# A hybrid RWKV-7 / pooling / mixture-of-experts step on one core: the chunk inverses' first level taken by ScalarE instead of VectorE, the key norms taken one number a token, and the state factors as one product a direction

## The reference, cut to what matters

```
kk    = heads(k * k_k);  kk = kk / max(sqrt(sum(kk*kk, -1)), 1e-12)      # key norm, one number a token and head
k_dir = heads(k * (1 + (a - 1) * k_a))
step: sa = s @ kk_t;  s = s * w_t - sa (x) (kk_t * a_t) + v_t (x) k_t;  y = s @ r_t     # per head, both directions
y     = groupnorm(y_f + y_b) * ln_x_w + ln_x_b;  y = (y + bonus) * g
```

## Time and profile before

| | |
|---|---|
| median of 3 runs (lowest to highest) | 3024.35 us (3022.92 to 3027.27) |
| the profiled execution, its span | 3028.03 us, 3026.2 us |
| projection phase, scan phase | 0 to 406 us, 406 to 1167 us |
| output and routing, experts and end | 1167 to 1360 us, 1360 to 3026 us |
| busy over the span: PE, DVE, ACT, POOL | 90%, 40%, 19%, 19% |

### The profile page before, as it was taken

How to read it: one execution, slowest core, us unless ns; L and a number is a source line. 1 busy time by engine, 2 the same in 40 slices (tenths; PEclk the granted TensorE clock), 3 DMA queues, 4 the chain that set the end, 5 groups by cost and what they waited for, 6 DMA issues and landing times. The chain is left out here.

```text
span 3026.2 us, 74869 instructions
## 1 busy us (share of the span) xinstructions
PE 2715.8 (90%) x32716; PEld 2389.9 (79%) x32716; DVE 1214.7 (40%) x3032; ACT 568.8 (19%) x1406; POOL 569.1 (19%) x571
## 2 busy tenths in 40 slices
PE   7999947788878897976999999999999999999991
PEld 2555527777767883446999999999999999999991
DVE  1488565757575453324223321332123222332125
ACT  4010153444342232320000100010000100010002
POOL 0693024534444331000000000000000000000002
PEclk9999979999999998987999999999999999999996
DMA  5522210000001004017687768777787768777753
GB/s 205 165 98 83 84 39 7 3 4 7 4 5 39 5 5 172 28 40 283 259 319 279 266 249 295 265 277 272 253 305 281 272 242 318 271 265 259 279 210 133
DMA packets 235257, 517.92 MB, mean 171 GB/s; under 512 B 9853, under 2 KB 42877, under 8 KB 234938
## 3 DMA queue, kind: packets, MB, share of 16 engines
q1 hardware_dynamic: 224410, 483.14, 43.3%
q0 software_dynamic: 8176, 21.83, 3.0%
q10 hardware_dynamic: 2480, 10.06, 0.8%
HBM read 488.68 MB, written 26.33 MB: 170 GB/s over the span
## 5 line engine op out<-in xcount | busy, mean ns | idle before, releaser
L2275 PE MATMUL ps_h<-xT,w1c 128*128 128x144 f32 x4096 | 547.1, 287 | 1.3 <-ACT xT L2081 1.3
L2275 PE MATMUL ps_h<-xT,w3c 128*128 128x144 f32 x4096 | 544.3, 286 | 0.0
L2275 PEld LDWEIGHTS ps_h<-xT,w1c 128*128 128x128 f32 x4096 | 520.4, 191 | 1.7 <-ACT xT L2081 1.7
L2275 PEld LDWEIGHTS ps_h<-xT,w3c 128*128 128x128 f32 x4096 | 519.9, 190 | 0.0
L2285 PE MATMUL ps_ye<-he,w2c 128*128 128x144 f32 x4096 | 512.3, 286 | 0.0
L2285 PEld LDWEIGHTS ps_ye<-he,w2c 128*128 128x128 f32 x4096 | 505.9, 190 | 0.0
L2230 DVE TENSOR_TENSOR u<-ps_h,sig 128x144 f32<-128x144 f32 x256 | 78.8, 308 | 887.8 <-ACT sig L2112 887.8
L563 PE MATMUL front_bank<-wide,win 128*128 128x384 f32 x912 | 298.9, 490 | 2.0 <-DVE wide L447 2.0
L563 PEld LDWEIGHTS front_bank<-wide,win 128*128 128x128 f32 x912 | 173.8, 191 | 128.2 <-issue 9.9
L2112 ACT ACTIVATE sig<-ps_h 128x144 f32<-128x144 f32 x256 | 74.4, 291 | 1065.8 <-PE ps_h L2275 1065.8
L2143 POOL DMA_INDIRECT acc<-ys,idx_s x16 | 25.8, 1615 | 1002.8 <-ACT ye_p L2101 872.0
(11 more groups left out here) (292 smaller groups left out, 3176.1 us busy)
## 6 DMA issues: line engine op xcount, KB each, us to landing
w1c<-in_w SPq DMA_DIRECT2D x64, 2048.0 KB, 8.1
w3c<-in_w SPq DMA_DIRECT2D x64, 2048.0 KB, 13.0
w2c<-in_w SPq DMA_DIRECT2D x64, 2048.0 KB, 13.4
ada<-in_ada_w SPq DMA_DIRECT2D x24, 1024.0 KB, 6.0
prow<-probsT ACTq DMA_DIRECT2D x17, 576.0 KB, 7.2
...
```

The source lines that it names most:

```text
L2275: ins = eng.matmul(ps_h[g % 2][:, off:off + SLOTS], w[:, b, k, f * P:(f + 1) * P], xT[:, k], start=(k == 0), stop=(k == KT - 1))
```

## The change

Five things, all in the scan phase (the experts' phase only has two counters merged into one).

1. Level 0 of the inverse: GpSimd's `begin_tt` now adds the identity to `lm` in place, one pair ahead, right behind `level(n, 0)`. TensorE's product with the identity then is T whole. ScalarE copies it (`begin_t`) and the transpose (its own `begin_tt`) to `tw`; VectorE's `take_t(n, 0)` is gone.
2. The key norm: a job `ks` a tile multiplies the squares as stationary operand with one column of ones (36 matmuls with one moving column), so that sums stand as 128x9 for each head; two small square roots, then `invert` (floor and reciprocal of 128x18). A job `kb` a piece (12 matmuls of 64x64) spreads the result back over rows and columns, and VectorE's `unit` reads it from PSUM in two products of 128x3x64, and does the product with the rates as before. `unit` runs in the job's spot.
3. `factors` is one product of 128x20 a direction; `rk_b` is gone.
4. The reciprocal of `spread` is three of 128x128.
5. The tables: `ks`, `w`, `a`, `kb` and the norm's jobs at other spots, with a fifth spot (k = 4) at the end of a pair; `exps` and GpSimd's `kr` one place earlier.

```diff
         def jobs(p, k):            # excerpts
-            for lo, name, t in ((0, "w", 0), (3, "a", 0), (6, "kk", 0), (9, "w", 1)):
+            for lo, num, name, t in ((0, 1, "ks", 0), (1, 3, "w", 0), (4, 3, "a", 0), (7, 3, "kb", 0), (10, 3, "w", 1)):
...
-            for name, spots in (("a", ((0, 3), (1, 0), (1, 1))), ("kk", ((1, 2), (1, 3), (2, 0))),
-                                ("bonus", ((3, 1), (3, 2), (3, 3)))):
+            spots = {"ks": ((0, 0),), "w": ((0, 1), (0, 2), (0, 3)) if t > 1 else (), "a": ((1, 0), (1, 1), (1, 2)),
+                     "kb": ((1, 3), (2, 0), (2, 1)), "bonus": ((3, 1), (3, 2), (3, 3))}
...
     @block.gpsimd
         def begin_tt(n):
-            eng.wait_ge(lm_p[n % 2], levels_done(n, 0))
-            if n >= 2:
-                eng.wait_ge(wu_pe, n - 1)
-            eng.tensor_tensor(tw[:, n % 2, :, 1], lm[:, n % 2, 0],
+            eng.wait_ge(lm_p[n % 2], levels_done(n, 0) - 1)
+            eng.tensor_tensor(lm[:, n % 2, 0], lm[:, n % 2, 0],
                               eye.unsqueeze(1).to_broadcast([P, 4, CH]), ALU.add).then_inc(lm_p[n % 2], 1)
...
-                if (r, q) in ((2, 5), (3, 1), (3, 3)):
-                    kr(t, ((2, 5), (3, 1), (3, 3)).index((r, q)))
+                if (r, q) in ((2, 4), (3, 0), (3, 2)):
+                    kr(t, ((2, 4), (3, 0), (3, 2)).index((r, q)))
...
     @block.scalar
+        def begin_t(n):
+            b = n % 2
+            if n >= 2:
+                eng.wait_ge(wu_pe, n - 1)
+            eng.wait_ge(x_pe[b], (n // 2) * LEVELS + 1)
+            eng.activation(tw[:, b, :, 0], INV[b][:, 0:4 * CH].rearrange("p (u c) -> p u c", u=4), ACT.Copy).then_inc(t0_s[b], 1)
+
+        def begin_tt(n):
+            b = n % 2
+            eng.wait_ge(lm_p[b], levels_done(n, 0))
+            eng.activation(tw[:, b, :, 1], lm[:, b, 0], ACT.Copy).then_inc(t0_s[b], 1)
...
-                spots = ((2, 3), (2, 4), (2, 5), (3, 1), (3, 2), (3, 3))
+                spots = ((2, 2), (2, 3), (2, 4), (2, 5), (3, 1), (3, 2))
...
-            for n in old:
-                take_wu(n)
+            begin_t(a)
+            if old:
+                take_wu(old[0])
+            begin_t(a + 1)
+            begin_tt(a)
+            if old:
+                take_wu(old[1])
+            begin_tt(a + 1)
...
     @block.vector
+        def invert(t):
+            eng.wait_ge(job_s, taken[("ks", t, 0)])
+            eng.tensor_scalar(rt[:], rt[:], 1e-12, None, ALU.max).then_inc(par_v, 1)
+            eng.wait_ge(par_v, 2 * t + 3)
+            eng.reciprocal(rt[:], rt[:]).then_inc(par_v, 1)
...
-            x = kr[:, 1, 1, piece(c)]
-            eng.reciprocal(x, x).then_inc(unit_v, 1)
-            eng.wait_ge(unit_v, 9 * t + 3 * c + 1)
-            eng.scalar_tensor_tensor(kx, kx, head(t, "k_k"), x, ALU.mult, ALU.mult).then_inc(unit_v, 1)
+            eng.wait_ge(job_p, order_pe[("kb", t, c)])
+            k3 = kx.rearrange("p (b c x) -> p b c x", c=2, x=CH)
+            for m, b in enumerate(bank_of("kb", t, c)):
+                eng.scalar_tensor_tensor(k3[:, :, m], k3[:, :, m], head(t, "k_k"), b[:, 0:PIECE // 2].rearrange("p (b x) -> p b x", x=CH),
+                                         ALU.mult, ALU.mult).then_inc(job_v, 1)
...
-            take_t(a, 0)
-            take_t(a + 1, 0)
...
-                if (r, q) in ((1, 5), (2, 1), (2, 4)):
-                    floor(t, ((1, 5), (2, 1), (2, 4)).index((r, q)))
-                if r == 2 and q in (2, 3, 5):
-                    unit(t, (2, 3, 5).index(q))
+                if (r, q) == (0, 5):
+                    invert(t)
...
     @block.tensor
+            elif name == "ks":
+                eng.wait_ge(square_s, 3 * t + 3)
+                for j in range(NCH):
+                    for h in range(2):
+                        ins = mm(b[h][H[j % 2], j // 2:j // 2 + 1], squares(t)[H[h], j * CH:(j + 1) * CH], blk[H[h], h * HS:h * HS + 1])
+            elif name == "kb":
+                eng.wait_ge(par_v, 2 * t + 4)
+                for j in range(NB // 3):
+                    for m in range(2):
+                        for h in range(2):
+                            i = c * (NB // 3) + j
+                            ins = mm(b[m][H[h], j * CH:(j + 1) * CH], rt[H[m], h, i:i + 1].to_broadcast([HS, HS]), eye[H[m]])
```

More of the change, by code:

```diff
@@ L673, in scan_phase @@
     t_v = [sem(f"t_v{i}") for i in range(2)]
+    t0_s = [sem(f"t0_s{i}") for i in range(2)]
     f_v = sem("f_v")
@@ L717, in chunk, with factor @@
     def chunk(n, d, c):
-        return 2 * where(n, d)[1] + c
+        j = 2 * where(n, d)[1] + c
+        return j + (1 if j < 2 else 2)
+    def factor(n, d, c):
+        return chunk(n, d, c) - d
     def in_step(d, k):
@@ L801, in scan_phase, with job_banks @@
                 order_pe[job] = len(order_pe) + 1
-    assert len(order_pe) == 7 * CT * 3
-    def job_banks(p, k, name):
+    assert len(order_pe) == 7 * CT * 3 + CT
+    def job_banks(p, k, job):
         if p == -1:
@@ L809, in job_banks @@
             return [G[k % 4]]
-        return [G[1]] if name in ("bonus", "gate") else G[0:2]
+        if k == 4:
+            return [G[2 + jobs(p, k).index(job)]]
+        return [G[1]] if job[0] in ("bonus", "gate") else G[0:2]
     spot_of = {job: (p, k) for p in range(-1, TAIL + 1) for k in range(spots_of(p)) for job in jobs(p, k)}
@@ L931, in between @@
                 r = p - base
-                spots = ((2, 0), (2, 1), (5 if t < 2 else 3, 0))
+                spots = ((2, 1), (2, 3), (3, 2))
                 if (r, q) in spots:
@@ L941, in _ @@
             level(n, 0)
+            begin_tt(n)
             level(n, 1)
@@ L946, in _ @@
             a = 2 * p
-            begin_tt(a)
-            begin_tt(a + 1)
             between(p, 0)
@@ L1077, in spot @@
                     rate(t, c)
-                if name in ("kk", "var"):
+                if name in ("ks", "var"):
                     root(name, t, c)
@@ L1083, in between @@
                 r = p - base
-                if (r, q) in ((1, 3), (1, 4)):
-                    for c in ((0,), (1, 2))[q - 3]:
-                        square(t, c)
-                spots = ((2, 3), (2, 4), (2, 5), (3, 1), (3, 2), (3, 3))
+                if r == 0 and q <= 3:
+                    square(t, q - 1)
+                spots = ((2, 2), (2, 3), (2, 4), (2, 5), (3, 1), (3, 2))
                 if (r, q) in spots:
@@ L1094, in between @@
                 r = p - base
-                spots = ((0, 5), (1, 1), (3, 5) if t < 2 else (2, 1))
+                spots = ((0, 5), (1, 1), (2, 3))
                 if (r, q) in spots:
@@ L1100, in _ @@
             square(0, c)
-        eng.wait_ge(par_v, 1)
-        for k in range(9):
+        eng.wait_ge(par_v, 2)
+        for k in range(10):
             spot(-1, k)
@@ L1107, in _ @@
         centres(0)
-        for k in range(9, 12):
+        for k in range(10, 13):
             spot(-1, k)
@@ L1177, in centre @@
             for d in range(2):
-                s3 = sums[d].rearrange("p (n c) -> p n c", c=CH)
-                eng.tensor_tensor(s3, s3, ht[:, t % 2, d, jc].unsqueeze(2).to_broadcast([P, NC, CH]),
-                                  ALU.subtract).then_inc(span_v, 1)
+                for lo, hi, at in parts:
+                    s3 = sums[d].rearrange("p (n c) -> p n c", c=CH)[:, lo:hi]
+                    ins = eng.tensor_tensor(s3, s3, ht[:, d, at + lo:at + hi].unsqueeze(2).to_broadcast([P, hi - lo, CH]), ALU.subtract)
+                ins.then_inc(span_v, 1)
             own = (kr[:, 0, 0, piece(c)], kh[:, 1, piece(c)])
@@ L1208, in spread @@
             eng.wait_ge(job_s, taken[("var", t, c)])
-            eng.reciprocal(x, x).then_inc(spread_v, 1)
+            for j in range(3):
+                ins = eng.reciprocal(x[:, j * P:(j + 1) * P], x[:, j * P:(j + 1) * P])
+            ins.then_inc(spread_v, 1)
         def keys(t, c):
@@ L1309, in take_job @@
         def take_job(name, t, c):
-            if name in ("w", "a", "kk", "var"):
+            if name in ("w", "a", "ks", "var"):
+                return
+            if name == "kb":
+                unit(t, c)
                 return
@@ L1352, in _ @@
             centre(0, c)
-        for c in range(3):
-            floor(0, c)
-        for c in range(3):
-            unit(0, c)
+        for k in range(7, 10):
+            spot(-1, k)
         for c in range(3):
@@ L1597, in spot @@
                     eng.wait_ge(d_s, 2 * p + 2)
+            else:
+                eng.wait_ge(am_v, min(2 * p + 4, NCELL))
             for name, t, c in jobs(p, k):
                 job(p, k, name, t, c)
-        for k in range(12):
+        for k in range(13):
             spot(-1, k)
```

164 lines of the change are left out of this document (78 added, 86 removed).

## The result

The changed kernel takes 3014.15 us (median of 8 runs, 3010.21 to 3018.82), the kernel before, run beside it, 3027.09: a ratio of 0.9957, 95% interval 0.9947 to 0.9968, or 13 us less. The forecast was 23 less. The profiled execution has 3018.82 us with a span of 3016.4, 9.8 less than the span before; the scan phase is 750.3 long instead of 760.6, and the rest is unchanged (1858.8 and 1858.9).

What follows compares the result with a forecast made beforehand. TensorE was taken to bound undisturbed scan pairs, its waits and their clock echo the pairs preparing a tile, VectorE the prologue. Terms summed to -23.1 us, from 3028.0 to 3004.9 (3001 by the median); 8-in-10 range 2986 to 3015.

Steps and rivals of the forecast that it cites:

- Prologue: Before the pairs: VectorE loses reciprocals and floors, partly offset by table loads and `keys` beside `kr`: -4 us (-1 to -8).
- Pair 0: In pair 0, `begin_tt` moves ahead of three `bonus`, so TensorE's wait of 5.53 shrinks: -4 us (0 to -5.5).
- ScalarE's chain: At pair starts, ScalarE's added copies delay `xw`; slack of 1.2 covers all but about 0.1 a pair: +1.7 us.
- rival C: At pair starts, ScalarE's four operations take 0.8 instead of 0.38 each, making the kernel slower: 3030 us, chance 0.07.
- Level-0 waits: At level 0 of pairs other than 0, all TensorE waits for VectorE's level 0 go: -16.1 us.
- What is given back: In pairs 2, 6, 10, `unit` of two pieces ahead of the last `take_t` costs +6.3 us (0 to +12).
- Level 4 of pairs 3, 7, 11: VectorE is 4 early there, but GpSimd's `kr` ahead of level 4 is late next: -7 us (0 to -12).
- Jobs: TensorE's `ks` and `kb` jobs replace `kk` jobs in the pairs: +3 us (-3 to +8).
- table loads: Table loads of 1.28 around `ks` in pairs 4 and 8, partly hidden: +1 us.
- Clock: Where waits of 3 to 5 us shrink in three pairs, some lower-clock time comes back: -4 us (0 to -12).
- the forecast's own case: Over the whole kernel, the terms sum to -23.1 us, with own range 2992 to 3009 us; chance 0.50.
- rival A: At pair ends `unit` costs 12, and level 4 wins only 2 waiting for `kr`: -12.4, 3012 us, chance 0.20.

Runs made afterwards that it cites:

- e1: The kernel before with only part 1 of the change (level 0 of the inverse) and two counters merged with others: 0.9968 of the kernel before.
- e12: The changed kernel with `ks` at 4 matmuls instead of 36 and a copy for the square root in tiles 1 to 3: 0.9931 of the kernel before.
- e6: The changed kernel with its level-0 part undone, all else as changed: 0.9963 of the kernel before.
- e15: The changed kernel with the last piece of GpSimd's `kr` one place later and the level-0 part undone: 0.9886 of the kernel before.
- e11: The changed kernel with only the last piece of GpSimd's `kr` one place later, behind level 4's masks in pairs 3, 7, 11: 0.9897 of the kernel before.
- e9: The changed kernel with GpSimd's addition of the identity done on one column of each 64x64 block instead of 64: 0.9939 of the kernel before.
- e4: The changed kernel with the wide product of `unit` moved behind the last `take_t` of the pairs: 0.9940 of the kernel before.
- e2: The changed kernel with `exps` and GpSimd's `kr` back at their old places, one place later each: 0.9941 of the kernel before.

## Why the direction was right and the size wrong

**Prologue**, -4: measured 3.86 (53.72 to 49.86). VectorE's `keys` took 2.55 each beside `kr`, as taken. **Pair 0**, -4: 2.7 in the changed kernel, 4.9 in e1, which has no `ks`, and in e12, which cuts it short. The wait of 5.53 went.

**ScalarE's chain**, +1.7: the mechanism held, and there was next to nothing to pay. ScalarE and TensorE in pair 12, which starts at 927.30:

```profile
931.28 0.42 ACT L1060 ACTIVATE tw<-lm 128x256 f32<-128x256 f32 x1
931.58 0.66 ACT L1064 ACTIVATE xw<-bank 128x256 f32<-128x256 f32 x2
...
932.16 0.31 PE L1438 MATMUL bank<-xw,tw 64*64 64x64 f32 x4
```

The copy from SBUF takes 0.42, `xw` starts at +4.3 (+3.4 in the earlier trace rows) and TensorE uses it at +4.9 (+5.0 there). So the slack pays for it, rival C's 0.8 a copy is out, and pairs 12 to 16 have 167.4 us instead of 169.6.

**Level-0 waits**, -16.1: they went, and the sum has them once, so the 10 us that are missing don't lie here. What the step had wrong is what they are owed to: it gave all of them to the level-0 part. e6 has 4.5 of them left without that part: the two parts removed the same queue, and with the key norm changed the move is worth nothing that can be measured (e15 against e11). In pair 11 the reciprocal of `spread`, a term put at 0, was 2.5 of that queue.

**What is given back**, +6.3, at most +12: the step that failed first. Pairs 2, 6, 10 are 16.3 us longer (5.8, 2.8, 7.7), and still 9.9 longer together with 1, 5 and 9, which got 6.4 shorter and for which there was no term (some of the jobs' +3 is in this). Of the waits for the last `take_t`, forecast at 2 us for the starts of pairs 3, 7 and 11, only pair 3 has one (2.1); the longer ones, 3.0 and 3.8 (1.4 and 1.7 before), stand at pairs 2 and 6, behind `centre`. And the clock, which the step left out, fell in these pairs. Pair 2 before and after:

```profile
532.17:565.80 33.63, 28.74 (x996) 27.07 (x997) 27.04 (x54) 16.14 (x39) 11.15 (x14) 1.00 0.02 4
...
524.94:564.35 39.41, 33.32 (x1040) 31.68 (x1041) 22.82 (x52) 16.93 (x48) 14.95 (x16) 0.88 0.01 4
```

Of its 5.8 us more, 4.6 are TensorE's busy time, with 44 records more at a lower clock. The two products of `unit` took 404 ns each, not the 276 that half of 551 makes, and the wide one 1.36 instead of 1.025 on the mean of tiles 1 and 3, and it stands ahead of evictions too. The step also said that GpSimd's addition "moves to where it sat idle". It was idle, but VectorE was not: e9 puts 5 to 8 us on that. e4 puts 5 to 8 on the wide product. The waits for `xw` of level 3, 2.1, 2.25 and 1.5 in these pairs, are for the most part not from early `exps`: the kernel before has 1.7, 1.7 and 1.3 one level on, and e2 2.0, 2.0 and 1.6.

**Level 4 of pairs 3, 7, 11**, -7: the mechanism was read rightly (`kr` ahead of level 4, GpSimd late next, the bonus job early), its price was not. The step had level 4 some 3 late; it was 4.4, and by e11 that costs 20.3 us in three pairs, with the clock. The pairs still got 15.8 shorter, together with their starts. With the last `kr` left behind level 4 they get 36 shorter: the step never asked what the short VectorE queue would give without the earlier `kr`.

**Jobs**, +3, and **table loads**, +1: pairs 4 and 8 are 5.9 longer, and e12 gives at most 8 to 11 for all of it. The records of `ks` took half of the 2.1 that the sum has, by the 29 ns of a product with two combinations of halves; part of the rest is the pause within it, which no row of before could show. **Clock**, -4: nothing came back. Pair 7 went from 0.89 to 0.92, but pair 2 from 1.00 to 0.88, and the window of all pairs has 0.96 as before. In pairs 3, 7 and 11 it came back in full in e11, at 8.3 us.

So the forecast's own case was not what happened; rival A's size (-12.4) was. A named both places, the pairs with `unit` and the wait for `kr`, with other amounts: it had 12 given back and 2 won at level 4, where pairs 2, 6, 10 show 16.3 more and, as an estimate, 4.6 won at level 4 and after it (15.8 less the three long waits for level 0, 11.2). Pairs 1, 5, 9 and everything from pair 12 on got 6.4 and 3.7 shorter, which neither had. That the whole comes out near A's sum, and that 3014 lies inside the range, is in part luck. What stays open: how e12's gain divides into `ks`, its pause, its echo in the clock and the pairs from 12 on; how the 16.3 divides, since e4 and e9 have 5 to 8 each and e6, without the level-0 part, still has 9.0; and which of e2's late `exps` and late first two `kr` makes its bonus jobs late, as no run has them apart.
